# Small column tiles for the recurrence's levels in a two-layer hybrid encoder

## The chip, the cores and the metric

The kernel runs on one core of one Trainium2 chip. The metric is the device time of one execution in microseconds (us), as the median of a number of runs. The engines of the core are TensorE (matmul, in the profile as PE, its weight loads as PEld), VectorE (DVE), ScalarE (ACT), GpSimd (POOL) and SyncE (SP), which issues most transfers.

## The reference

The model has two layers over 512 tokens of width 1024, all in float32. Each layer mixes tokens in two groups of heads and then runs a gated convolutional feed-forward part:

```python
h = rms_norm(x, mix_norm_g[l])
proj = h @ w_in[l]                       # 1024 -> 4096
y_a = diff_attention(...)                # 4 heads, (softmax1 - lambda * softmax2) V
y_b = hgrn2_bidirectional(...)           # 4 heads, state 128 x 128, forward and backward
x = x + concat(y_a, y_b) @ w_out[l]
x = x + conv_glu_ffn(rms_norm(x, ffn_norm_g[l]), ...)   # 1024 -> 5632 -> 2816 -> 1024
```

The change is in the recurrence `y_b`. With forget gates f, keys k, values v and queries q per token it computes

```python
S_t = diag(f_t) S_{t-1} + k_t v_t^T ;  o_t = S_t^T q_t      # and the same backward, summed
```

Within a block of 128 tokens this is a matrix of scores A[s, t], in which key s and query t are multiplied with all forget gates that lie between them, and then A times v.

## The kernel before

**Columns.** A projection is cut into units: 128 output columns, a weight tile of 128 x 1024 in `raw`. ScalarE rounds it to `wH` (`high_now`, L893), POOL subtracts to get the rest `wL` (`split`, L491, in four pieces), and TensorE adds three products for each of the 8 slices (`triple`, L559 to L561): 24 matmuls of 128 x 512 a unit. `raw`, `wH` and `wL` have two buffers, so the split of unit s+1 is made while TensorE works on unit s, and unit s+1 can't start before it.

**Slots.** The mixing part of a layer is one hand-written list of 40 slots (L800). In each slot TensorE does, in this order: an item of the recurrence, the scores of an attention step, the first half of a unit's columns, then transposes of the attention weights W (`turn`, L717), the second half, a statistic (L609) and the attention's product with V (`values`, L726). Each other engine walks the same slots in an order of its own, and all wait on semaphores.

**The recurrence.** Heads go in pairs. A pair has 12 items, from slot 7 (pair 0) and slot 19 (pair 1). Item 0 computes the diagonal of A. Items 1 to 7 are levels: at level lv blocks of h = 2^(lv-1) tokens are joined in twos, and only the entries of A between two neighbouring blocks are new. For each level TensorE multiplies, for 2 heads and 4 blocks of 128 tokens, the keys `kx` (128 x 128, stationary) with the queries `QQ` (128 x 128, moving), which fills a bank of PSUM for each head (`item`, L612; L639 for the diagonal, L647 for h = 1, L650 for the other levels). Of the 128 x 128 results only the entries of a mask are kept.

Behind an item:
- POOL (`grow`, L505) waits for its last matmul (`lv_mm`), multiplies the totals (L518) and the keys KK (L524), and only then splits the next unit's weights (L491).
- ScalarE copies the grown keys to `kx` for the next level (L994).
- VectorE copies the masked entries to A (`masked`, L1394) and grows the queries QQ (L1415; at level 1 also the totals, L1424). In the same slot it takes a unit's result from PSUM (L1307), does the maximum of the scores (L1452), the weights W (`combine`, L1458 to L1463), squares (L1342) and rotary and norm work (L1319 to L1337).
- The next item waits for the queries (`hg_q`), the keys (`kx_ready`) and the masked copy (`a_msk`).

Items 8 to 11 turn the keys, carry the state from block to block and add all up (`to_keys`, `carry`, `gather`). The scores of the attention (`scores`, L708) are products of 64 rows: the two halves of the array hold the two softmaxes.

Of the kernel before, what the change touches and what calls it, by code (L numbers as in the profile page):

```python
# [11 lines left out]
ACT = mybir.ActivationFunctionType  # L12
AX = mybir.AxisListType

P = 128
D = 1024
S = 512
DEPTH = 2
HEADS = 4
# [2 lines left out]
EPS = 1e-6  # L22
KT = D // P
TT = S // P
FT = DFF // P


UNIT = KT * P
N_IN, N_OUT, N_UP, N_DOWN = 32, 8, 2 * FT, FT
U_OUT = N_IN  # L30
# [4 lines left out]

ROWS = FT - 4
U_TAIL = U_DOWN + ROWS
# [101 lines left out]
R_CONV = 26  # L139
NR = R_CONV + 8 * (FT + 2)  # L140

# [24 lines left out]
def build(nc, xT, wts, cst, msk, par, lbl, pos, outT):  # L166
# [15 lines left out]
    with ctx:  # L182
# [29 lines left out]
        KK = sb("KK", [P, 2, HEADS * S], F32, mix)  # L212
        A = sb("A", [P, 2, TT, P], F32, mix)
        KTOK = sb("KTOK", [P, 2, 2, TT - 1, P], F32, mix)
        ST = sb("ST", [P, 2, 2, TT - 1, P], F32, mix)
        QQ = sb("QQ", [P, 2, HEADS * S], F32, mix)
        T = sb("T", [P, 2, HEADS * S], F32, mix)
        HI = sb("HI", [P, TT, S], F32, mix)
        V = sb("V", [P, TT, S], F32, mix)
        QO = sb("QO", [P, HEADS, S], F32, mix)  # L220
        K2 = sb("K2", [P, 2, S], F32, mix)
        E = sb("E", [P, 2, S], F32, mix)
        wT = sb("wT", [P, 2, TT, P], F32, mix)
        kx = sb("kx", [P, 2, S], F32, mix)
# [6 lines left out]
        heads.close()  # L231
        gH = sb("gH", [P, FT * S], F32R, ffn)
        gL = sb("gL", [P, FT * S], F32R, ffn)
# [44 lines left out]
        kx_ready = signal("kx_ready", 14)  # L278
# [83 lines left out]

            return t[:, s, c * UNIT // 2:(c + 1) * UNIT // 2]

        def crossing(t, hd, i, h, left, n=1):


            side = HEADS * S * (1 if left == 0 else -1)
            return bass.AP(tensor=t[:].tensor, offset=left * HEADS * S + hd * S + i * P,
                           ap=[[2 * HEADS * S, P], [2 * h, n * P // (2 * h)], [side + h, 2], [1, h]])  # L370

        def neighbours(t, hd, i):


            return bass.AP(tensor=t[:].tensor, offset=hd * S + i * P,
                           ap=[[2 * HEADS * S, P], [HEADS * S + 1, 2], [2, P // 2]])

        def conv(p, c, n):

# [45 lines left out]
        with nc.Block() as block:  # L425
# [129 lines left out]
            def _(pe):  # L555
                for l in range(DEPTH):
# [55 lines left out]
                    def item(n):  # L612

                        pair, lv = divmod(n, PAIR_ITEMS)
                        if lv in (TURN_F, TURN_B):
                            to_keys(pair, lv - TURN_F)
                        if lv == CARRY:
                            carry(pair, 0)
                        if lv >= LEVELS:
                            return  # L620
                        pe.wait_ge(*hg_q.at(l, 9 * pair + lv + 1))
                        if lv:
                            pe.wait_ge(*kx_ready.at(l, 7 * pair + lv))
                        elif n == 0:
                            pe.wait_ge(*lam_exp.at(l, 1))
                        for r in range(2):
                            hd, b = 2 * pair + r, bank[2 + r]

                            if lv == 0:
                                if pair:  # L630
                                    pe.wait_ge(*oh_ready.at(l, r + 1))
                            elif lv == 1:
                                pe.wait_ge(*a_cp.at(l, 2 * pair + r + 1))
                            else:
                                pe.wait_ge(*a_msk.at(l, 14 * pair + 2 * (lv - 2) + r + 1))
                            for i in range(TT):
                                o = b[:, i * P:i * P + P]
                                if lv == 0:
                                    m = pe.matmul(o, kx[:, r, i * P:i * P + P], head(QQ, 1, hd, i, 1),  # L639
                                                  start=True, stop=True)  # L640
                                else:

                                    h = 2 ** (lv - 1)
                                    if h == 1:
                                        m = pe.matmul(o.rearrange("p (n two) -> p two n", two=2), kx[:, r, i * P:i * P + P],  # L647
                                                      neighbours(QQ, hd, i), start=True, stop=True)
                                        continue
                                    m = pe.matmul(o.rearrange("p (n two h) -> p n two h", two=2, h=h),  # L650
                                                  kx[:, r, i * P:i * P + P], crossing(QQ, hd, i, h, 0),
                                                  start=True, stop=True)
                            m.then_inc(lv_mm.sem, 1)

                    def to_keys(pair, d):
# [144 lines left out]
                    for s in range(SLOTS):  # L800
                        n = item_of(s)
# [60 lines left out]
                    for j in range(4):  # L862
                        pe.wait_ge(*w_split.at(l, U_TAIL + j + 1))
                        for c in range(2):
                            for k in range(4):
                                at = slice((ROWS + k) * S, (ROWS + k + 1) * S)
                                m = triple(bank[2 * j + c][:], j % 2, (2 * k + c) * P, gH[:, at], gL[:, at], False, k == 3)
# [3 lines left out]
            def _(act):  # L871
# [14 lines left out]
                for l in range(DEPTH):  # L886
# [83 lines left out]
                    def item(n):  # L970

                        pair, lv = divmod(n, PAIR_ITEMS)
                        if lv == 0:
                            for r in range(2):
                                act.wait_ge(*lv_mm.at(l, 16 * pair + r + 1))
                                if pair:
                                    act.wait_ge(*av_mm.at(l, r + 1))
                                act.activation(diag(r), bank[2 + r][:].rearrange("p (i t) -> p i t", i=TT), ACT.Copy)\
                                   .then_inc(a_cp.sem, 1)
                        if lv in (TURN_F, TURN_B):  # L980
                            d = lv - TURN_F
                            for r in range(2):
                                act.wait_ge(*kt_mm.at(l, 4 * pair + 2 * d + r + 1))
                                if pair:
                                    act.wait_ge(*kv_mm.at(l, 2 * d + r + 1))
                                act.activation(KTOK[:, r, d, :, :].rearrange("p n c -> p (n c)"), bank[2 + r][:, 0:3 * P], ACT.Copy)\
                                   .then_inc(kt_ready.sem, 1)
                        if lv <= 6:

                            act.wait_ge(*lv_mm.at(l, 16 * pair + 2 * lv + 2))  # L990
                            if lv:
                                act.wait_ge(*hg_k.at(l, 7 * pair + lv))
                            h = 2 ** lv
                            act.activation(kx[:].rearrange("p r t -> p (r t)").rearrange("p (n two h) -> p n two h", two=2, h=h),  # L994
                                           crossing(KK, 2 * pair, 0, h, 0, 2 * TT), ACT.Copy).then_inc(kx_ready.sem, 1)

                    def recurrent_out(pair):

# [647 lines left out]
```

## Time and profile before

| | us |
|---|---|
| median of 3 runs | 1389.43 (1387.84 to 1389.66) |
| the profiled execution | 1387.78 |
| its span | 1386.0 |
| TensorE busy in the span | 1369.8 |
| VectorE busy | 925.8 |
| POOL busy | 705.2 |
| ScalarE busy | 628.1 |

The profile is of one execution. Its span goes from the first to the last instruction; 1.78 us of the execution's time lie around it. Matmuls overlap each other, so the mean duration of one (390 ns for 512 columns of results) is longer than the step from one to the next. Busy shares are means over stages with different limits.

### The profile page before, as it was taken

The page shows a single profiled execution, that of the slowest core. Times are in us where ns is not written, and L with a number is a line of the kernel's source. Part 1 is how long each engine was busy: PE and PEld are TensorE (multiplying, and loading weights), DVE is VectorE, ACT ScalarE, POOL GpSimd, SP SyncE. Part 2 cuts the span into 40 slices and gives each one's busy share as a digit, 9 for nine tenths or more (in the row PEclk, how much of TensorE's full clock was granted, in tenths as well). Part 3 has the DMA queues.
Part 4 walks back from the last instruction along what each step waited for, and adds up shares of the span by engine and source line. Part 5 has one row for each costly group of instructions (what it writes and reads, how often), then busy time and mean ns, then how long its engine had stood idle before and what let it go on. Part 6 is the DMA issues. An engine that isn't in the chain of part 4 may idle for free.

```text
span 1386.0 us, 18086 instructions
## 1 busy us (share of the span) xinstructions
PE 1369.8 (99%) x6562; PEld 1119.9 (81%) x6562; DVE 925.8 (67%) x1078; ACT 628.1 (45%) x912; POOL 705.2 (51%) x539
## 2 busy tenths in 40 slices
PE   9999999999999999999999999999999999999999
PEld 6887787877888888888878877878778888888887
DVE  7687899555888888600356788985558888885001
ACT  6343666474544444312444426655745444443121
POOL 2785465337444444444567845552464444444443
PEclk9999999999999999999999999999999999999999
DMA  5223112122233233233332221221223333233233
GB/s 187 77 74 102 46 55 76 47 73 95 92 92 106 91 96 102 92 104 97 91 92 76 92 69 49 69 74 46 63 89 107 92 93 105 91 100 98 91 104 109
DMA packets 37130, 121.36 MB, mean 88 GB/s; under 512 B 4928, under 2 KB 5440, under 8 KB 37056
## 3 DMA queue, kind: packets, MB, share of 16 engines
q1 hardware_dynamic: 36768, 119.84, 27.9%
q8 instruction: 47, 0.77, 0.2%
q10 hardware_dynamic: 288, 0.52, 0.1%
q14 instruction: 27, 0.22, 0.1%
HBM read 114.05 MB, written 2.10 MB: 84 GB/s over the span
## 4 chain that ended last, share of the span: by engine, by line
PE 83%; DVE 6%; POOL 4%; ACT 4%; issue 3%; DMA 0%; ACTq 0%; POOLq 0%; DVEq 0%
PE bank L559 24%; PE bank L561 24%; PE bank L560 24%; PE bank L650 2%; PE bank L708 2%; PE bank L726 2%; POOL wL L497 1%; POOL KK L524 1%; PE bank L717 1%; DVE hL L399 1%; POOL rstd L411 1%; PE bank L681 1%; POOL wL L491 1%; ACT wH L893 1%; PE bank L647 1%
## 5 line engine op out<-in xcount | busy, mean ns | idle before, releaser
L497 POOL TENSOR_TENSOR wL<-raw,wH 128x1024 fp32r<-128x1024 f32 x142 | 343.1, 2416 | 404.4 <-ACT wH L893 294.2
L559 PE MATMUL bank<-hH,wH 128*128 128x512 f32 x1216 | 483.1, 397 | 2.6 <-POOL wL L491 1.3
L561 PE MATMUL bank<-hL,wH 128*128 128x512 f32 x1216 | 474.4, 390 | 0.0
L560 PE MATMUL bank<-hH,wL 128*128 128x512 f32 x1216 | 473.7, 390 | 0.0
L491 POOL TENSOR_TENSOR wL<-raw,wH 128x256 fp32r<-128x256 f32 x268 | 240.1, 927 | 186.7 <-ACT wH L893 186.6
L559 PEld LDWEIGHTS bank<-hH,wH 128*128 128x128 f32 x1216 | 228.3, 188 | 66.4 <-issue 16.3
L561 PEld LDWEIGHTS bank<-hL,wH 128*128 128x128 f32 x1216 | 228.2, 188 | 48.7
L560 PEld LDWEIGHTS bank<-hH,wL 128*128 128x128 f32 x1216 | 228.6, 188 | 45.4 <-issue 0.5
L893 ACT ACTIVATE wH<-raw 128x1024 fp32r<-128x1024 f32 x173 | 182.6, 1055 | 154.4 <-PE bank L561 154.1
L1567 DVE TENSOR_TENSOR x<-x,bank 128x512 f32<-128x512 f32 x16 | 10.9, 683 | 200.7 <-PE bank L561 200.7
L559 PE MATMUL bank<-gH,wH 128*128 (+1 forms) x352 | 137.2, 390 | 0.0
L561 PE MATMUL bank<-gL,wH 128*128 (+1 forms) x352 | 136.9, 389 | 0.0
L560 PE MATMUL bank<-gH,wL 128*128 (+1 forms) x352 | 136.9, 389 | 0.0
L1554 DVE TENSOR_TENSOR gL<-gt,gH 128x512 fp32r<-128x512 f32 x44 | 99.6, 2264 | 30.8 <-ACT gH L1146 30.8
L1541 DVE SCALAR_TENSOR_TENSOR ua<-uu,R,ua 128x511 f32<-128x511 f32 x44 | 111.4, 2531 | 1.5
L901 ACT ACTIVATE wH<-raw 128x1024 fp32r<-128x1024 f32 x36 | 38.1, 1059 | 146.4 <-PE bank L561 146.4
L1135 ACT ACTIVATE ua<-uu,R 128x512 f32<-128x512 f32 x44 | 35.9, 816 | 126.8 <-DVE uu L1532 126.8
L1532 DVE TENSOR_TENSOR uu<-bank,rms 128x512 f32<-128x512 f32 x88 | 59.9, 684 | 44.9 <-PE bank L561 26.9
L524 POOL TENSOR_TENSOR KK<-KK,T 128x512 f32<-128x512 f32 x56 | 74.5, 1352 | 25.2 <-PE bank L647 25.2
L559 PEld LDWEIGHTS bank<-gH,wH 128*128 128x128 f32 x352 | 66.1, 188 | 14.5 <-issue 0.7
L561 PEld LDWEIGHTS bank<-gL,wH 128*128 128x128 f32 x352 | 66.1, 188 | 13.7
L560 PEld LDWEIGHTS bank<-gH,wL 128*128 128x128 f32 x352 | 66.1, 188 | 13.6
(173 smaller groups left out, 1801.2 us busy)
## 6 DMA issues: line engine op xcount, KB each, us to landing
raw<-wts SPq DMA_DIRECT2D x210, 512.0 KB, 3.5
x<-xT SPq DMA_DIRECT2D x8, 256.0 KB, 5.2
swp<-K SPq DMA_DIRECT2D x32, 64.0 KB, 2.0
swp<-QO SPq DMA_DIRECT2D x32, 64.0 KB, 2.2
outT<-x SPq DMA_DIRECT2D x8, 256.0 KB, 2.0
raw<-wts ACTq DMA_DIRECT2D x2, 256.0 KB, 4.4
raw<-wts SPq DMA_DIRECT2D x2, 256.0 KB, 5.4
W<-pos SPq DMA_DIRECT2D x1, 256.0 KB, 5.8
```

Source lines behind the costliest of these rows:

```text
L491: m = pool.tensor_tensor(wL[:, s, at], raw[:, s, at], wH[:, s, at].bitcast(F32), ALU.subtract)
L497: pool.tensor_tensor(wL[:, s, :], raw[:, s, :], wH[:, s, :].bitcast(F32), ALU.subtract)\
L524: last = pool.tensor_tensor(v, v, w.to_broadcast([P, n, h]), ALU.mult)
L559: pe.matmul(out, wH[:, s, a:a + P], rhs_h, start=first, stop=False)
L560: pe.matmul(out, wL[:, s, a:a + P], rhs_h, start=False, stop=False)
L561: return pe.matmul(out, wH[:, s, a:a + P], rhs_l, start=False, stop=last)
L893: act.activation(wH[:, u % 2, :], raw[:, u % 2, :], ACT.Copy).then_inc(w_high.sem, 1)
L901: act.activation(wH[:, s, :], raw[:, s, :], ACT.Copy).then_inc(w_high.sem, 1)
L1135: act.activation(dst[:, q, :], uu[:, q, c, :], ACT.Identity, bias=conv(p, c, 3), scale=conv(p, c, 1))\
L1532: dve.tensor_tensor(uu[:, p % 2, c, :], bank[(2 * p + c) % 4][:], rms[:], ALU.mult).then_inc(up_ev.sem, 1)
L1541: dve.scalar_tensor_tensor(dst[:, q, 0:S - 1], uu[:, q, c, 1:S], conv(p, c, 2), dst[:, q, 0:S - 1], ALU.mult, ALU.add).then_inc(conv_done. ...
L1554: dve.tensor_tensor(gL[:, at], gt[:, p % 2, :], gH[:, at].bitcast(F32), ALU.subtract)\
```

## The change

For levels 1 to 7 each product of a 128 x 128 block is replaced by products of smaller blocks on the diagonal. Where the joined blocks (2h tokens) fit into 32 tokens, so for levels 1 to 5 (h = 1 to 16), there are four, each with 32 keys as stationary columns and 32 queries as moving columns; their results lie at PSUM partitions 0, 32, 64 and 96, so at four column quarters of the array. For level 6 (h = 32) there are two of 64 by 64, and for level 7 (h = 64) two of 64 by 64 off the diagonal: the keys of one half with the queries of the other. All contract over the 128 rows as before. The diagonal (item 0), the semaphores and the other engines' instructions stay; ScalarE's copy to `kx` calls the same helper with other arguments and does the same.

```diff
+SUB, QUARTER = P // 2, P // 4
...
-        def crossing(t, hd, i, h, left, n=1):
+        def crossing(t, hd, i, h, left, g=None):
             side = HEADS * S * (1 if left == 0 else -1)
-            return bass.AP(tensor=t[:].tensor, offset=left * HEADS * S + hd * S + i * P,
-                           ap=[[2 * HEADS * S, P], [2 * h, n * P // (2 * h)], [side + h, 2], [1, h]])
+            at, n = g or (0, 2 * S)
+            return bass.AP(tensor=t[:].tensor, offset=left * HEADS * S + hd * S + i * P + at,
+                           ap=[[2 * HEADS * S, P], [2 * h, n // (2 * h)], [side + h, 2], [1, h]])
-        def neighbours(t, hd, i):
-            return bass.AP(tensor=t[:].tensor, offset=hd * S + i * P,
-                           ap=[[2 * HEADS * S, P], [HEADS * S + 1, 2], [2, P // 2]])
+        def neighbours(t, hd, i, g):
+            return bass.AP(tensor=t[:].tensor, offset=hd * S + i * P + g * QUARTER,
+                           ap=[[2 * HEADS * S, P], [HEADS * S + 1, 2], [2, QUARTER // 2]])
+        def across(t, hd, i, g):
+            at = hd * S + i * P + g * SUB
+            return t[:, g, at:at + SUB]
...
-                                else:
-                                    h = 2 ** (lv - 1)
-                                    if h == 1:
-                                        m = pe.matmul(o.rearrange("p (n two) -> p two n", two=2), kx[:, r, i * P:i * P + P],
-                                                      neighbours(QQ, hd, i), start=True, stop=True)
-                                        continue
-                                    m = pe.matmul(o.rearrange("p (n two h) -> p n two h", two=2, h=h),
-                                                  kx[:, r, i * P:i * P + P], crossing(QQ, hd, i, h, 0),
-                                                  start=True, stop=True)
+                                    continue
+                                h = 2 ** (lv - 1)
+                                sub = QUARTER if 2 * h <= QUARTER else SUB
+                                for g in range(P // sub):
+                                    s, at = kx[:, r, i * P + g * sub:i * P + (g + 1) * sub], slice(g * sub, (g + 1) * sub)
+                                    if h == SUB:
+                                        m = pe.matmul(o[at, (1 - g) * SUB:(2 - g) * SUB], s, across(QQ, hd, i, 1 - g),
+                                                      start=True, stop=True)
+                                    elif h == 1:
+                                        m = pe.matmul(o[at, at].rearrange("p (n two) -> p two n", two=2), s,
+                                                      neighbours(QQ, hd, i, g), start=True, stop=True)
+                                    else:
+                                        m = pe.matmul(o[at, at].rearrange("p (n two h) -> p n two h", two=2, h=h), s,
+                                                      crossing(QQ, hd, i, h, 0, (g * sub, sub)), start=True, stop=True)
                             m.then_inc(lv_mm.sem, 1)
...
-                                           crossing(KK, 2 * pair, 0, h, 0, 2 * TT), ACT.Copy).then_inc(kx_ready.sem, 1)
+                                           crossing(KK, 2 * pair, 0, h, 0), ACT.Copy).then_inc(kx_ready.sem, 1)
```

## Rows read from the trace of the kernel before

**Rows 1.** The page: TensorE's busy time, share, instructions; the chain by engine.

```profile
PE 1369.8 (99%) x6562; PEld 1119.9 (81%) x6562; DVE 925.8 (67%) x1078; ACT 628.1 (45%) x912; POOL 705.2 (51%) x539
...
PE 83%; DVE 6%; POOL 4%; ACT 4%; issue 3%; DMA 0%; ACTq 0%; POOLq 0%; DVEq 0%
```

**Rows 2.** One line's instructions: durations in ns, minimum, median, maximum.

```profile
L650 PE MATMUL bank<-QQ,kx x384: 270/275/348, 61.5 to 910.3; 128*128 128x128 f32 x192
```

**Rows 3.** TensorE's timeline, level 5 of pair 0: start us, duration us.

```profile
85.32 0.39 PE L561 MATMUL bank<-hL,wH 128*128 128x512 f32 x1
85.55 1.95 PE L650 MATMUL bank<-QQ,kx 128*128 128x128 f32 x16
...
87.57 0.40 PE L560 MATMUL bank<-hH,wL 128*128 128x512 f32 x1
```

**Rows 4.** Timeline at an L708; counts in 0.04 us (TensorE, loads).

```profile
146.43 0.28 PE L639 MATMUL bank<-QQ,kx 128*128 128x128 f32 x1
146.64 0.70 PE L708 MATMUL bank<-K,QO 64*128 64x512 f32 x2
...
148.04 0.40 PE L560 MATMUL bank<-hH,wL 128*128 128x512 f32 x1
...
146.63:146.66 0.03, 0.02 (x2) 0.02 (x2) 1.00 0.47 137
...
147.16:147.20 0.04, 0.04 (x4) 0.00 (x0) 1.00 0.86 205
```

**Rows 5.** Timeline at L573, and its durations in ns.

```profile
22.71 1.02 PE L568 MATMUL bank<-rstd,C 128*128 128x512 f32 x2
23.57 0.28 PE L573 MATMUL bank<-lamc,C 128*128 128x2 f32 x2
...
L573 PE MATMUL bank<-lamc,C x4: 167/209/251, 23.6 to 710.8; 128*128 128x2 f32 x4
```

**Rows 6.** L650's weight loads; TensorE's first stand for the split.

```profile
L650 PEld LDWEIGHTS bank<-QQ,kx x384: 186/192/192, 61.3 to 910.2; 128*128 128x128 f32 x192
...
63.98 0.47 PE L559 MATMUL bank<-hH,wH 128*128 128x512 f32 x1 [0.39 <-POOL wL L491]
```

**Rows 7.** POOL's timeline, pair 0; its waits to 102: us, times, longest.

```profile
56.26 3.45 POOL L524 TENSOR_TENSOR KK<-KK,T 128x512 f32<-128x512 f32 x2 [3.13 <-PE bank L647]
59.67 4.16 POOL L491 TENSOR_TENSOR wL<-raw,wH 128x256 fp32r<-128x256 f32 x4
63.78 1.67 POOL L518 TENSOR_TENSOR T<-T 128x256 f32<-128x256 f32 x2
...
68.41 2.81 POOL L491 TENSOR_TENSOR wL<-raw,wH 128x256 fp32r<-128x256 f32 x4
...
POOL T L518 <- PE bank L650: 2.8, 3, 1.5
```

**Rows 8.** The same waits in layer 1, from 743 to 783.

```profile
POOL T L518 <- PE bank L650: 4.1, 4, 1.5
```

**Rows 9.** A slot of pair 1: length, busy PE, PEld, DVE, ACT, POOL; clock.

```profile
165.90:177.20 11.30, 10.70 (x60) 8.22 (x60) 11.09 (x17) 6.18 (x11) 7.14 (x8) 1.00 0.27 80
```

**Rows 10.** Waits: VectorE from 156.3 to 223.5, TensorE from 158.3 to 221.3.

```profile
DVE sm L1452 <- PE bank L708: 0.7, 2, 0.3
...
DVE A L1394 <- PE bank L650: 0.2, 1, 0.2
...
PE bank L717 <- DVE W L1463: 0.3, 1, 0.3
```

**Rows 11.** W made ready on VectorE and turned on TensorE, pair 1's level 5.

```profile
203.32 1.11 DVE L1463 SCALAR_TENSOR_TENSOR W<-E,sm 128x512 f32<-128x512 f32 x1
...
204.66 0.60 PE L717 MATMUL bank<-C,W 128*128 128x128 f32 x4
```

**Rows 12.** The weights' transfers: count, KB each, us to landing.

```profile
raw<-wts SPq DMA_DIRECT2D x210, 512.0 KB, 3.5
```

**Rows 13.** TensorE's longest waits in layer 1, columns as in rows 9.

```profile
815.00:823.00 8.00, 5.38 (x27) 3.50 (x26) 7.61 (x21) 3.43 (x7) 1.24 (x2) 1.00 0.26 87
```

## The prediction, made before the changed kernel was run

> **What bounds the kernel now.** I read the shares and the chain of waits first, then TensorE's groups by form, its order of time around single items, and then POOL and VectorE in the stretches in which the recurrence runs. TensorE is busy for 99% of the span and has 83% of the chain [rows 1]: time taken from it shortens the kernel, unless another engine is late there. The changed products are 384 of the 6562 TensorE records under L650, 192 products in two records each [rows 2]: 2 layers, 2 pairs of heads, levels 2 to 7, 8 products. Level 1 adds 64 under L647. So an item (one level of one pair) is 8 products in 16 records. Its price is read from the steady matmuls about it, not from the duration of 275 ns, since matmuls overlap: the last column matmul before it starts at 85.32, the second after it at 87.57; with 0.23 for each column matmul the item takes 87.57 - 0.23 - 85.55 = 1.79 us [rows 3]. That is 0.11 a record. The 28 items of levels 1 to 7 are 50 us, 3.6% of the span of 1386.0; 20 of them become quarters, 8 halves.
>
> **What replaces an item.** A quarter item issues four products of 128 rows, 32 columns and 32 tokens for each old one: 64 weight loads and 64 matmuls. A half item issues 32 and 32. Nothing before shows a column tile, so I bound it.
> - Below: the four quarters run side by side and each takes a matmul in 28 ns. That is the start-to-start of L573's two matmuls of 2 columns: the pair covers 0.28 us and the second alone 0.251 [rows 5]. 16 in each quarter are 0.45 us.
> - Middle: the quarters take turns, 64 x 0.028 = 1.79 us: what it was.
> - Above: each small pair costs what a whole one does, 64 x 0.11 = 7.0 us.
>
> The nearest row for the choice is L708, the two half-height products of the scores (64 rows each): two matmuls of 0.69 us each start together and are both over in 0.70, and both second passes start in the same 0.04 us [rows 4]. Tiles of the array do run side by side for float32, and two loads and two matmuls go out within 0.03 us, so issue is no bound of 28 ns either. I take the lower bound plus a third for 128 instructions: 0.6 us. Halves: 16 in each half at half of 0.11, 0.9 us.
>
> **Switches of tiling.** They are in the trace, at L708. In: L639's last matmul starts at 146.43 and would leave the array after 0.11; L708 starts at 146.64, 0.10 later than that [rows 4]; and a first weight load then lies bare, 0.1 for 128 columns, 0.02 for 32. Out: the second pass starts at 147.18, is worth 0.43 (two take 23.57 - 22.71 [rows 5]), and L560 starts at 148.04 where 147.18 + 0.43 + 0.23 = 147.84 was due: 0.20. So a quarter item pays 0.12 in and 0.20 out. In pair 1 the scores follow at once and L708 pays its switch today already, so only 0.12 is new.
>
> The Trainium skill says the same of the switch ("TensorEngine Tiling (Array Packing)", Key Properties: a change of tiling mode drains TensorE), and its section Instruction Overhead warns against taking the tiling factor from a dimension that is small already, since a matmul with few columns lasts as long as one with 60. Here the moving size falls from 128 to 32, so that rule speaks against this change: its figure of 60 cycles gives an estimate of 0.025 us for each of 64, 1.6 us in turn. By it the item gains nothing; side by side the same floor gives 0.4.
>
> **Sum on TensorE alone.** Pair 0: quarter item 0.12 + 0.6 + 0.20 = 0.92, saves 0.87, five times; half item 0.12 + 0.9 + 0.20 = 1.22, saves 0.57, twice: 5.5 us a layer. Pair 1: 0.72 and 1.02, saves 1.07 and 0.77: 6.9 a layer. Both layers: 24.8 us. I don't expect it, because two other engines are just behind.
>
> **Pair 0: POOL.** In each slot POOL waits for the item's last matmul, grows the keys, then splits the next unit's weights, for which TensorE waits. In layer 0 POOL runs without a gap from 56.26 (released by L647) to 71.2, and TensorE stands for the split at 63.98 and once more, at 79.52 [rows 6, 7]: grow and split take 63.78 - 56.26 = 7.5 us there, a slot's 24 column matmuls 24 x 0.227 = 5.45. With items of 0.9 TensorE's slot is 6.4 and POOL sets the pace. What POOL gives back: the start after item 1 (about 1.0 earlier) and its three gaps, 2.8 us with 1.53 the longest [rows 7]: 3.8 us at most. Stepping both engines through levels 1 to 7 with POOL's durations kept, TensorE reaches the columns after level 7 3.6 us early. In layer 1 there are four gaps, 4.1 us [rows 8], and the same stepping gives 3.6. POOL's splits take 2.8 us alone and up to 4.2 beside VectorE [rows 7, 8]; filled gaps mean more overlap, so I take 3.4 a layer, 6.8. ScalarE's copies to kx come ready before the columns end, at level 3 up to 0.3 after; that is in the stepping.
>
> **Pair 1: VectorE.** Of five slots of 10.3 to 11.3 us VectorE is busy in each for all but 0.1 to 0.6 (11.09 of 11.30 in the fullest, records overlapping a little [rows 9]). From 156.3 to 223.5 it waits 1.1 us in all, at the two ends, and TensorE waits for its W once [rows 10]. An item shorter by 1.07 makes TensorE's slot 9.3 to 9.7, less than VectorE's work. What can move: VectorE's two waits at the head, 0.17 before L1394 and 0.33 before L1452, so some 0.5; then the products are turned (L717) as soon as W is ready, and for the turn at 204.66 W was done at 204.43, a slack of 0.2 [rows 11]. There TensorE can be 0.7 early. The two half items behind add 0.77 each while VectorE gets back 0.16 + 0.34, the like two waits behind level 7 [rows 10]; the turn at 235.00 has its W at 233.97, 1.0 before. So min(0.7 + 1.5, 1.05 + 1.0) = 2.0 us a layer, 4.0 in all; the other 9.8 become waits before L717 and the items. Behind that VectorE has gaps of several us and TensorE is the bound again, so what is gained by then stays.
>
> In layer 1 VectorE is also full between pair 0's last level and the first scores, and TensorE stands still there for 2.6 of 8 us [rows 13]; that work starts from level 7's item and moves with it, so I subtract nothing. PSUM's other columns hold old sums, which the masks leave out; VectorE, POOL and ScalarE have the same instructions. Weight transfers land after 3.5 us [rows 12] and are asked for a slot of about 7 us ahead; they stay hidden. The granted clock is 1.00 (2.4 GHz) even in those 8 us [rows 13], and the new waits are shorter.
>
> **Sum.** 6.8 + 4.0 = 10.8 us. The profiled execution took 1387.78, span 1386.0 and 1.78 about it; it becomes 1377.0. The median of the runs, 1389.43, lies 1.65 above it: predicted 1378.6. The result's own range: with items of 0.8 and POOL not slowed, 13.5 less (1376); with items of 1.2 and each bound tighter by a third, 7 less (1382.5).
>
> **Rivals.**
> - Quarters take turns. A quarter item is 1.79 + 0.12 + 0.20 = 2.11, a half item (32 x 0.056) + 0.32 the same: 0.32 more than before in pair 0, 0.12 in pair 1. Pair 0: seven items 2.2, of which 0.2 falls into TensorE's waits for the split; pair 1: 0.8. A layer 2.9, in all 5.8: 1395.2, slower. It decides from 23 ns for a small pair counted over all quarters: (1.79 - 0.32) / 64. For it: the quarters read the same 128 rows, L708's halves different ones. Against: the overlap at L708. 15%.
> - A small pair costs what a whole one does or nearly: items of 3.5 to 7.2. All 28 at 1.7 more are 48 us: 1437; at 5.3 more, over 1500. For it: 0.11 is the step of every run of pairs in the rows. Against: L573's 28 ns. 5%, 2 of them for this: where a load can't lie beside a matmul of the same rows, a pair is 0.11 / 4 + 0.028 and an item 3.5. The Trainium skill has that as a rule ("TensorE: Matmul & The Clock Gate", The mechanism: loads overlap matmuls only in another row group). The trace speaks against it: L650's loads last 0.19 each at a step of 0.11 beside matmuls of the same rows [rows 2, 6].
> - Overlap of two instead of four (both bounds met half way): quarter item 0.12 + 1.0 + 0.20, saves 0.47 in pair 0 and 0.67 in pair 1. POOL and VectorE then bind less: 1.7 and 1.2 a layer, in all 5.8: 1383.6. 9%.
> - It does run side by side, but the other engines give back nearly nothing (POOL slowed by what the gaps gave): within 3 us, 1387. 5%.
>
> **How the numbers follow.** Forecast 66%, the rivals 15, 5, 9 and 5. 0.2% is 2.8 us, about what can be told from no change. Faster: 66 + 8 of the third, 1 of the fourth, less 3 for what I overlooked, 72%. Same: 10%. Slower: 13 of the first, 5 of the second: 18%. The likeliest's own range is 1376 to 1382.5; the range of all reaches over the third, fourth and first: 1374.5 to 1396.
>
> **What would show it.** Starts of small matmuls under the new lines 7 to 10 ns apart across quarters, an item of 0.7 to 0.9 us from last column matmul to next; POOL without gaps from level 1 to 6 of pair 0, and TensorE waiting for wL (L491) in five or six slots a layer instead of one or two; in pair 1 new waits of TensorE for VectorE (W, QQ, A). The prediction is wrong if items are over 1.5 us, if a clock under 1.00 shows there, or if VectorE's work turns out to shrink.

## The result, and the profile after

| | before | changed |
|---|---|---|
| median of the runs, us | 1388.64 (4 runs, 1387.84 to 1389.66) | 1376.32 (4 runs, 1375.31 to 1377.66) |
| ratio, 95% interval | | 0.9911 (0.9894 to 0.9929) |
| profiled execution, us | 1387.78 | 1376.25 |
| its span, us | 1386.0 | 1374.5 |
| mean granted clock | 1.000 | 0.998 |

The kernel became 12.3 us faster by the medians and 11.5 by the spans of the profiles; 10.8 was forecast, and 1378.6 as the time. Lines of the changed kernel stand 7 to 9 further down than in the kernel before: the column matmuls at L566 to L568 (L559 to L561), `to_tokens` at L601 (L594), the scores at L717 (L708), the turn of W at L726 (L717). Some experiments shift them once more. First the page of the changed kernel, the lines that answer to [rows 1]:

```profile
PE 1346.1 (98%) x7650; PEld 1091.3 (79%) x7650; DVE 918.4 (67%) x1078; ACT 628.6 (46%) x912; POOL 709.3 (52%) x539
...
PE 72%; DVE 13%; POOL 5%; issue 5%; ACT 4%; DMA 0%; DVEq 0%; ACTq 0%; POOLq 0%
```

TensorE has 1088 instructions more and 23.7 us of busy time less; half of that is in the span. The rest has become waits: 13% of the chain lies on VectorE instead of 6%. POOL and VectorE have as many instructions as before, but VectorE's take 7.4 us less in all.

**The item.** TensorE's timeline at a quarter item (level 5 of pair 0, to be held against [rows 3]) and at a half item (level 7 of pair 0). Columns: start us, duration us.

```profile
83.87 0.39 PE L568 MATMUL bank<-hL,wH 128*128 128x512 f32 x1
84.19 0.76 PE L660 MATMUL bank<-QQ,kx 128*32 128x32 f32 x64
84.88 0.51 PE L566 MATMUL bank<-hH,wH 128*128 128x512 f32 x1
85.22 0.39 PE L567 MATMUL bank<-hH,wL 128*128 128x512 f32 x1
...
97.99 0.40 PE L617 MATMUL bank<-sqR,meanR 128*128 128x512 f32 x1
98.31 1.15 PE L654 MATMUL bank<-QQ,kx 128*64 128x64 f32 x32
99.40 0.50 PE L566 MATMUL bank<-hH,wH 128*128 128x512 f32 x1
99.73 0.39 PE L567 MATMUL bank<-hH,wL 128*128 128x512 f32 x1
```

By the prediction's own way of reading, the quarter item takes 85.22 - 0.23 - (83.87 + 0.23) = 0.89 us (1.79 before, 0.92 forecast) and the half item 99.73 - 0.23 - (97.99 + 0.23) = 1.28 (1.22 forecast). The switch in is 84.19 - 84.10 = 0.09; the first small matmul starts there, and the 64 starts cover 0.567 us, which is 9.0 ns from one to the next and 36 in each quarter, on the mean. In the first half of the item the trace has them in rounds: four starts 6 to 7 ns apart, one for each quarter, and the next four 32 ns after them (53 ns at the very first round); in the second half the order is less regular, about 34 ns for four. The 32 starts of a half item cover 0.93 us, 30 ns each.

**Pair 0.** POOL's waits, in layer 0 from 54.4 to 99 and in layer 1 from 735 to 780, to be held against [rows 7, 8] (us in total, times, longest):

```profile
POOL KK L531 <- PE bank L657: 2.0, 1, 2.0
POOL T L525 <- PE bank L660: 0.6, 2, 0.5
...
POOL T L525 <- PE bank L660: 1.7, 2, 1.0
```

The gaps of 2.8 and 4.1 us between POOL's levels have shrunk to 0.6 and 1.7. In exchange TensorE waits, in the whole span:

```profile
PE bank L566 <- POOL wL L498: 6.1, 6, 1.4
PE bank L601 <- DVE ev L1316: 3.7, 7, 1.2
PE bank L717 <- DVE QO L1334: 3.7, 2, 1.8
PE bank L726 <- DVE W L1472: 2.4, 2, 1.2
```

The first of them (1.3 us before) is the split of pair 0. The second, but for 0.3 us that was there before, and the third are VectorE in pair 1; before the change TensorE waited 0.3 us a layer there for QO and never for `ev`. L601 is `to_tokens`, for which VectorE takes the projection from PSUM to `ev` (L1316); QO is the rotated query of the attention's scores. The wait for W, which the prediction named, has gone down from 3.1 to 2.4 us, and in pair 1 from 0.3 us a layer to nothing.

**Pair 1.** VectorE has one wait of 0.2 us in the 81.4 us from 150.6 to 232 (busy 80.02). TensorE's timeline at the longest of its waits there, and two stretches in the columns of [rows 9] (length, busy PE, PEld, DVE, ACT, POOL, granted clock), one in each layer:

```profile
164.13 1.39 PE L717 MATMUL bank<-K,QO 64*128 64x512 f32 x4 [1.83 <-DVE QO L1334]
165.45 0.80 PE L566 MATMUL bank<-hH,wH 128*128 128x512 f32 x1
166.04 0.63 PE L567 MATMUL bank<-hH,wL 128*128 128x512 f32 x1
166.47 0.63 PE L568 MATMUL bank<-hL,wH 128*128 128x512 f32 x1
...
168.47 0.39 PE L567 MATMUL bank<-hH,wL 128*128 128x512 f32 x1
...
164.90:168.30 3.40, 3.40 (x9) 2.27 (x8) 3.33 (x3) 2.08 (x3) 3.40 (x4) 0.50 0.31 77
847.50:850.90 3.40, 3.40 (x8) 1.61 (x9) 3.29 (x5) 1.41 (x3) 3.40 (x4) 0.51 0.23 58
```

TensorE stands for 1.83 us, and behind that the granted clock is half (1.2 GHz instead of 2.4) for 3.41 us: column matmuls start 0.43 apart instead of 0.23. The same is found in layer 1.

**Stage by stage.** The start of TensorE's first matmul of a stage in the trace after, less that before:

| stage | shift at its start | at its end | the stage | forecast |
|---|---|---|---|---|
| pair 0, layer 0 | +0.21 | -3.36 | -3.57 | -3.4 |
| pair 1, layer 0 | -3.36 | -5.69 | -2.33 | -2.0 |
| pair 0, layer 1 | -5.77 | -9.16 | -3.39 | -3.4 |
| pair 1, layer 1 | -9.16 | -11.50 | -2.34 | -2.0 |

Between and behind these stages nothing moves by more than 0.1 us. The 0.2 us ahead of the first belong to the program's start, where TensorE's first waits differ.

**How the runs scatter.** Some executions of the kernel before take 1389.3 to 1389.7 us (mean clock 0.999), the others 1387.4 to 1388.2 (1.000). No trace of the first kind is kept of this very kernel; in before_mask1's, which took 1389.20, the clock falls once, in the middle of layer 1, behind a stand (the last section shows it). So its median moves by up to 1.5 us with the mixture. Medians below are set against 1387.95 (19 runs, for the first four experiments), 1387.93 (15, the next four), 1389.32 (7, the next three) and 1388.14 (3, the last). Where it matters I compare two traces instead, by how far the starts of TensorE's matmuls shift over a stage.

### The profile page after: what moved, and what is told of

The parts are those of the page before. It is cut to its first block, busy times and chain, and to the rows that moved or that the text cites. A ratio compares the mean times of both kernels' runs of the same rounds, so it can differ in the third digit from the quotient of the medians.

```text
span 1374.5 us, 20262 instructions
## 1 busy us (share of the span) xinstructions
PE 1346.1 (98%) x7650; PEld 1091.3 (79%) x7650; DVE 918.4 (67%) x1078; ACT 628.6 (46%) x912; POOL 709.3 (52%) x539
## 4 chain that ended last, share of the span: by engine, by line
PE 72%; DVE 13%; POOL 5%; issue 5%; ACT 4%; DMA 0%; DVEq 0%; ACTq 0%; POOLq 0%
PE bank L566 22%; PE bank L568 22%; PE bank L567 22%; DVE QQ L1424 2%; POOL KK L531 2%; POOL wL L504 1%; DVE A L1403 1%; DVE sm L1461 1%; POOL wL L498 1%; DVE E L1469 1%; PE bank L717 1%; DVE sqR L1351 1%; DVE hL L406 1%; DVE tmp L1328 1%; DVE swp L1330 1%
## 5 line engine op out<-in xcount | busy, mean ns | idle before, releaser
L566 PE MATMUL bank<-hH,wH 128*128 128x512 f32 x1216 | 484.3, 398 | 8.7 <-POOL wL L498 6.1
L568 PE MATMUL bank<-hL,wH 128*128 128x512 f32 x1216 | 475.0, 391 | 0.0
L566 PEld LDWEIGHTS bank<-hH,wH 128*128 128x128 f32 x1216 | 228.9, 188 | 73.0 <-issue 16.0
L568 PEld LDWEIGHTS bank<-hL,wH 128*128 128x128 f32 x1216 | 228.7, 188 | 49.3
L566 PE MATMUL bank<-gH,wH 128*128 (+1 forms) x352 | 137.2, 390 | 0.0
L568 PE MATMUL bank<-gL,wH 128*128 (+1 forms) x352 | 136.9, 389 | 0.0
L566 PEld LDWEIGHTS bank<-gH,wH 128*128 128x128 f32 x352 | 66.1, 188 | 14.3 <-issue 0.6
L568 PEld LDWEIGHTS bank<-gL,wH 128*128 128x128 f32 x352 | 66.1, 188 | 13.9
```

What stands on the lines that cost most here:

```text
L566: pe.matmul(out, wH[:, s, a:a + P], rhs_h, start=first, stop=False)
L568: return pe.matmul(out, wH[:, s, a:a + P], rhs_l, start=False, stop=last)
```

## The experiments

**Do the quarters run side by side?** same_quarter gives all four products of a block the same column quarter, and keeps their number and size (the sums of the levels are not the reference's); the half items stay as they are:

```diff
-    m = pe.matmul(o[at, at].rearrange(...), s, crossing(QQ, hd, i, h, 0, (g * sub, sub)), ...)
+    m = pe.matmul(o[0:sub, at].rearrange(...), s, crossing(QQ, hd, i, h, 0, (g * sub, sub)), ...)   # levels 1 to 5
```

> Built on the changed kernel. All four small products of a block at levels 1 to 5 write to PSUM partitions 0 to 31, so all use one column quarter of the array; count, sizes and order of the instructions stay. Their results overwrite what the masks would keep, so the levels' sums are left out. Theory (the quarters run side by side, 36 ns a pair in each, 64 x 9 ns in all): in one quarter 64 pairs follow each other at about 36 ns (28 at the least), an item's starts cover 1.8 to 2.3 us instead of 0.57, items grow by 1.2 to 1.7 us, and the kernel is no faster than the one before: 1388 to 1396. Rival (the price of a small pair is one of issue, 9 ns wherever it goes): items stay at 0.57 and the time at 1376.

quarter_by_quarter keeps the quarters, but issues the four blocks of one quarter behind each other, so that 8 records of a quarter follow each other. The same loop puts the records of the half items in rows of 8 of one half:

```diff
-    for i in range(TT):
-        for g in range(P // sub):
+    for g in range(P // sub):
+        for i in range(TT):
```

> Built on the changed kernel. Same products, another order: for each head first the four blocks of quarter 0, then those of quarter 1, and so on, so that 8 pairs (16 instructions) of one quarter stand in a row. Theory A (TensorE looks far enough ahead to feed four quarters from such a row): items 0.6 to 0.8 us of starts, time 1376 to 1378. Theory B (matmuls start in the order of the program, so a quarter's row must end before the next begins): starts 64 x 28 to 36 ns, 1.8 to 2.3 us, time 1388 or more. In the changed kernel two pairs of a quarter stand in a row already and cost nothing.

Measured: 1390.0 us (ratio 1.0011, 1.0000 to 1.0022) and 1382.75 (0.9957, 0.9941 to 0.9972). TensorE's timeline at level 5 of pair 0, first same_quarter, then quarter_by_quarter:

```profile
86.62 2.21 PE L660 MATMUL bank<-QQ,kx 128*32 128x32 f32 x64
88.76 0.50 PE L566 MATMUL bank<-hH,wH 128*128 128x512 f32 x1
```

```profile
84.87 1.51 PE L661 MATMUL bank<-QQ,kx 128*32 128x32 f32 x64
86.31 0.50 PE L566 MATMUL bank<-hH,wH 128*128 128x512 f32 x1
```

Same work, three prices: the 64 starts cover 2.02 us in one quarter (32 ns each), 1.32 in four with eight of one quarter in a row (21 ns), and 0.567 in turn (9.0 ns). The gain of the quarter items is overlap between quarters and nothing else: without it the kernel is no faster than before. In a row of one quarter the starts are 32 ns apart (the first two 53), and from round to round in the changed kernel they are 32 to 34: three neighbours hardly slow a quarter down.

The second run lies between the two theories. If records of different quarters overlapped freely wherever they stand in the program, it would be as fast as the change. Its starts show how far the overlap reaches: a row of 8 begins 0.153 us behind the one before it, 6 ns after the fifth record of that row, when three are still to start. So here quarters overlapped over the last three records of a row, and no further. Part of this run's loss is that of the half items: in rows of one half their starts cover 1.32 us instead of 0.93.

**What each part brings.** pair0_only leaves pair 1 the whole products, halves_only leaves them to levels 1 to 5 of both pairs:

```diff
     sub = QUARTER if 2 * h <= QUARTER else SUB
+    if pair == 1:        # pair0_only
+    if lv <= 5:          # halves_only
+        sub = P
```

> Built on the changed kernel. Pair 1's levels are whole products as before, pair 0's are small. Theory (pair 0 gives 3.57 and 3.39 us in the two layers up to POOL's pace, pair 1's part is its own): 7.0 us less than the kernel before, 1381.7, and the granted clock stays at 1.00 in pair 1's level 2, since TensorE's item is long enough that it doesn't stand before the scores. Rival (an earlier pair 0 moves VectorE's and POOL's work so that pair 1 gives or takes too): 5 or less, or 9 or more.

> Built on the changed kernel. Levels 1 to 5 are whole products as before, levels 6 and 7 are halves. Theory: a half item takes 1.1 us instead of 1.79 (0.7 less in pair 0, where both switches of tiling are new, 0.8 less in pair 1). In pair 0 POOL has 1.5 us to give behind level 5, so both items count: 1.4; in pair 1 VectorE is late by 0.5 at the most behind level 5, both count: 1.6. 3.0 a layer, 5 to 6 in all: 1383. Rival (behind level 5 the split's or VectorE's lateness takes one of the two): 3 in all, 1386.

Measured: 1382.13 us (0.9953, 0.9931 to 0.9976) and 1384.13 (0.9970, 0.9959 to 0.9981). With pair 0 alone the two stages bring 3.56 and 3.34 us, as in the change (3.57 and 3.39), pair 1 has its old waits of 0.3 us, and its clock stays at 1.00. So the two pairs add up: the trace is 6.9 us shorter than that of the kernel before, where 7.0 were expected. The medians say 5.8; two of this kernel's three runs have a mean clock of 0.999. The half items alone bring 2.0 us a layer, 0.8 in pair 0 and 1.2 in pair 1, where TensorE alone would give 1.0 and 1.6: less than the 3.0 of my theory and more than the rival's 1.5. Part of them is taken by the same two engines (POOL in pair 0, VectorE in pair 1: a wait of 0.2 before L601 is new).

**Is POOL the bound in pair 0?** after_split3 and before_split3 leave the last quarter of the split out for seven units of each layer, in pair 0's slots, in the changed kernel and in the one before (two of the 24 products of each of these units take an old wL there):

```diff
-    for q in range(4):
+    for q in range(3 if 9 <= u <= 15 else 4):
```

> Built on the changed kernel. POOL leaves out one of four pieces of the split for units 9 to 15, the ones split in pair 0's slots (a quarter of those units' low weights is stale). POOL is 0.9 to 1.0 us shorter in each of these slots. Theory (POOL sets the pace in pair 0: TensorE's seven items save 5.9 us a layer there and it keeps 3.4 to 3.6): most of the other 2.4 a layer comes back, 3.5 to 5 us less than the changed kernel: 1372. Rival (something else, the keys' copy on ScalarE or VectorE's queries, is late as well): under 1.5 us less.

> The same piece left out in the kernel before. There TensorE stands for the split three times, 0.39, 0.54 and 0.39 us. Theory: 1 to 1.5 us less than the kernel before, 1387.4. Rival (any POOL work taken off the stretch helps alike, also in the changed kernel): 4 us less here too.

Measured: 1372.91 us (0.9888, 0.9860 to 0.9917; two runs, the profiled one with a fall of the clock more than the change's) and 1385.75 (0.9983, 0.9972 to 0.9995). Against its own base the changed kernel gains 2.08 and 1.82 us in pair 0 of the two layers; the kernel before gains 0.8 and 0.2 there, and 1.2 more in layer 1, where TensorE's wait of 0.8 us before the carry goes. So the same relief of POOL is worth about 3.9 us in pair 0 after the change and 1.0 before: POOL, a near bound before, is the bound now. Both theories were a little off: 3.4 us by the medians of the changed kernel for the 3.5 to 5 expected, 2.2 in the kernel before for 1 to 1.5, still about half of the rival's 4.

**Is VectorE the bound in pair 1?** after_mask1 and before_mask1 copy only one block of four from PSUM to A in pair 1 (three quarters of the levels' entries of A are missing there), so that the two copies of 0.69 us in each slot take 0.25 each:

```diff
-    dve.copy_predicated(diag(r), m, bank[2 + r][:].rearrange("p (i t) -> p i t", i=TT))
+    dve.copy_predicated(diag(r)[:, 0:nb, :], m, ...[:, 0:nb, :])      # nb = 1 if pair else TT
```

> Built on the changed kernel. VectorE's masked copies of pair 1 take one block of 128 tokens instead of four (three quarters of the scores of pair 1 stay those of the diagonal). VectorE is about 1.0 us shorter in each of seven slots. Theory (VectorE is without a gap from level 1 of pair 1 on and TensorE loses 4.9 us a layer to it, 1.1 of them through the clock that falls while it stands): 7 to 9 us less than the changed kernel, 1368; clock 1.00 throughout. Rival (the loss is one of contention or of the switches of tiling): under 2 us less.

> The same copies shortened in the kernel before, where TensorE waited for VectorE in pair 1 for 0.35 and 0.25 us a layer. Theory: 1 to 1.5 us less than the kernel before, 1387.3. Rival: as much as in the changed kernel.

Measured: 1374.75 us (0.9901, 0.9873 to 0.9930; two runs) and 1388.64 (0.9999, 0.9988 to 1.0011; one of its eight runs took 4894.24, for which there is no trace, and the median of the other seven is 1388.10). The kernel before doesn't move, as expected: there VectorE has slack. The changed one gains 1.1 us in pair 1 of layer 0 and 1.8 in layer 1, where a fall of the clock is missing; the fall in layer 0 stayed, at 165.6 us. 7 to 9 were expected, so the number is the rival's, under 2 us by the medians. My reckoning by busy time was wrong. VectorE's timeline at level 1 of pair 1, after_mask1 and then the changed kernel:

```profile
152.91 0.50 DVE L1404 COPY_PREDICATED A<-M,bank 128x128 f32<-128x128 uint8 x2
153.85 1.29 DVE L1462 TENSOR_REDUCE sm<-bank 128x1 f32<-128x512 f32 x2 [0.44 <-PE bank L717]
155.06 1.34 DVE L1351 TENSOR_TENSOR sqR<-sq,sqR 128x512 fp32r<-128x512 f32 x1
```

```profile
152.80 1.37 DVE L1403 COPY_PREDICATED A<-M,bank 128x512 f32<-128x512 uint8 x2
154.06 1.27 DVE L1461 TENSOR_REDUCE sm<-bank 128x1 f32<-128x512 f32 x2
155.25 1.04 DVE L1351 TENSOR_TENSOR sqR<-sq,sqR 128x512 fp32r<-128x512 f32 x1
```

The copies lose 0.87 us, but behind them VectorE waits 0.44 for the scores of this slot, and its next instruction is 0.30 longer. What is left at L1351's end is 0.0. The wait for QO is 1.83 us as before. What is shortened ahead of the scores' maximum is not on the path; that runs from the scores to the maximum, squares, queries, totals, rotary work and so to the next scores. VectorE is full, and yet only the work behind one point in each slot counts. The rival's cause, contention, has a part too: seven times 0.87 us is 6.1, but the busy time of the same VectorE instructions falls by only 4.5 us a layer.

**Work on that path, and its neighbour.** totals_pool moves the totals of level 1 of pair 1 from VectorE to POOL, behind its split; the result stays the same. They take 2.25 us on VectorE, just ahead of the rotary work. totals_both in addition moves the totals of level 2 of pair 0 the other way, from POOL to VectorE:

```diff
+    def pair_totals(pair):                      # POOL, called for pair 1 (item 1)
+        pool.wait_ge(*hg_q.at(l, 9 * pair + 3))
+        ...
+            nxt = pool.tensor_tensor(totals(pair, 2)[:, d, :], w[:, :, 0], w[:, :, 1], ALU.mult)
+        nxt.then_inc(tot_ready.sem, 1)
-    if lv == 1:                                 # VectorE
+    if lv == 1 and not pair:
```

> Built on the changed kernel, whole computation. The totals of level 1 of pair 1 (two products of 128 x 512, 2.25 us on VectorE) are made on POOL, behind its split, where it stands 2.06 us for TensorE's next item. What shortening the masked copies showed: work of VectorE ahead of the maximum of the scores gives little (its time went to a wait of 0.44 for the scores and to slower instructions beside POOL); these totals lie behind it, on the way to the rotated queries for which TensorE stands 1.83 us before the next scores. Theory (that way sets the time of the slot, and the fall of the clock follows from the stand): the 1.83 goes, the clock stays at 1.00 in level 2, and the later waits for ev (0.33 and 1.22) shrink: 2 to 3 us a layer, 1371 (1370 to 1373). Rival (POOL's longer work, 3 us or more in a gap of 2, makes the keys or the split late, or slows VectorE by as much): 0 to 1.5 us, 1375 or more.

> The same, and in pair 0 the totals of level 2 (1.67 us on POOL) are made on VectorE, which is busy for 4.6 of 8.2 us in that slot. Theory (POOL sets pair 0's pace): 1 to 1.5 us a layer less than with the totals of pair 1 alone, 1368.5. Rival (VectorE's own items behind, the next queries or the totals for level 3, become late): no more than 1 us in all, 1370 to 1371.

Measured: 1374.53 us (0.9898, 0.9882 to 0.9915) and 1373.89 (0.9892, 0.9875 to 0.9908). The first gains 0.95 us a layer in pair 1, not 2 to 3: the rival's range, though its time lies a little under the rival's 1375. VectorE's timeline ahead of the scores' QO, in totals_pool (with POOL's row for the same time behind it) and in the changed kernel:

```profile
158.25 1.22 DVE L1339 SCALAR_TENSOR_TENSOR tmp<-QO,R,cosT 128x512 f32<-128x512 f32 x1
159.51 1.11 DVE L1341 SCALAR_TENSOR_TENSOR swp<-swp,R,sinT 128x512 f32<-128x512 f32 x1
160.65 1.41 DVE L1343 TENSOR_TENSOR QO<-tmp,swp 128x512 f32<-128x512 f32 x1
162.10 1.41 DVE L1345 TENSOR_TENSOR QO<-QO,rstd 128x512 f32<-128x512 f32 x1
...
160.03 2.93 POOL L540 TENSOR_TENSOR T<-T 128x512 f32<-128x512 f32 x2
```

```profile
158.63 2.25 DVE L1433 TENSOR_TENSOR T<-T 128x512 f32<-128x512 f32 x2
160.81 0.74 DVE L1328 SCALAR_TENSOR_TENSOR tmp<-QO,R,cosT 128x512 f32<-128x512 f32 x1
161.58 0.75 DVE L1330 SCALAR_TENSOR_TENSOR swp<-swp,R,sinT 128x512 f32<-128x512 f32 x1
162.37 0.69 DVE L1332 TENSOR_TENSOR QO<-tmp,swp 128x512 f32<-128x512 f32 x1
163.09 0.99 DVE L1334 TENSOR_TENSOR QO<-QO,rstd 128x512 f32<-128x512 f32 x1
```

The four instructions take 5.15 us here and 3.17 in the changed kernel: 1.98 of the 2.25 us come back. They now start 2.6 us earlier, so that the first two run nearly all beside POOL's split (until 160.06) and the last two beside the totals; in the changed kernel POOL stands from 160.34 to 162.40. The second move adds 0.6 us a layer in pair 0, at the bound that after_split3 showed: about half of the theory's 1 to 1.5, and its 1368.5 was far off. It is the fastest version here with the whole computation, 2.4 us under the change by the medians.

**The stand at level 2 of pair 1.** level2_whole gives that one item of each layer the whole products back. after_split3_pair1 shortens the split for pair 1's units instead, made beside VectorE's work (two products of each of these units take an old wL again):

```diff
+    if pair == 1 and lv == 2:                   # level2_whole
+        sub = P
-    for q in range(4):                          # after_split3_pair1
+    for q in range(3 if 20 <= u <= 27 else 4):
```

> Built on the changed kernel, whole computation. Only level 2 of pair 1 is whole products again, so TensorE works 1.1 us longer there and stands 0.7 instead of 1.8 us before the scores. Theory (the fall of the clock to half in that slot, 3.4 us, follows from TensorE's stand and costs 1.1 us a layer, since the columns behind it run at half speed): the fall goes in both layers, 2 us less than the changed kernel, 1374.3. Rival (the fall comes for another reason, the small tiles' low activity over the whole stretch, or costs nothing since VectorE is late anyway): 1376 as it was.

> Built on the changed kernel. POOL leaves out one of four pieces of the split for units 20 to 27, the ones split beside pair 1's levels (a quarter of those units' low weights is stale). TensorE never waits for POOL there, and POOL stands for 1.4 to 4.8 us in each slot. Theory (VectorE sets the pace of pair 1 and is slowed by POOL's work beside it, about 0.4 us for each us: with the totals moved to POOL the four rotary instructions took 5.15 us instead of 3.17, which gave back what the move saved): with 1.0 to 1.2 us less of POOL in each of eight slots VectorE gains some 0.4 a slot, and 1 to 2 us a layer come off, 1373 (1371.5 to 1374.5). Rival (POOL isn't late there, so its work costs nothing): within 0.7 us of the changed kernel, or no more than the fall of the clock in level 2 explains (1.1 a layer).

Measured: 1376.1 us (0.9907, 0.9891 to 0.9924) and 1372.86 (0.9887, 0.9858 to 0.9916; two runs). TensorE's timeline at the same scores, first level2_whole, then after_split3_pair1:

```profile
163.78 1.13 PE L719 MATMUL bank<-K,QO 64*128 64x512 f32 x4 [0.33 <-DVE QO L1336]
164.83 0.50 PE L566 MATMUL bank<-hH,wH 128*128 128x512 f32 x1
```

```profile
163.64 1.13 PE L717 MATMUL bank<-K,QO 64*128 64x512 f32 x4 [1.32 <-DVE QO L1334]
...
166.43 0.39 PE L567 MATMUL bank<-hH,wL 128*128 128x512 f32 x1
```

The slower item costs nothing: the scores start 0.35 us earlier than in the change (0.1 of it comes from before the stage), since QO was what they waited for, and the clock stays up behind a stand of 0.33. The next item starts 1.3 us earlier. Of that 1.0 is given back at the next wait for `ev` (level 4) and 0.6 won again at the two waits behind it; 0.9 us a layer stay, no more. This trace has a fall elsewhere, at 812.3 us (1.5 us), so its time hardly differs from the change's; its one run at clock 1.000 took 1374.52, the change's 1375.31. The theory's mechanism held, a short stand and no fall behind it, but its 2 us didn't come: 0.2 us by the medians, 0.8 at equal clock.

In after_split3_pair1 the stand is 1.32 us and the clock stays up too. It gains 1.83 and 1.74 us a layer. From L717 to the eighth column matmul behind it the changed kernel loses 1.55 us by the clock (168.47 - 164.13 = 4.34 against 166.43 - 163.64 = 2.79), of which TensorE would otherwise wait 0.4 for W. So at that place the fall costs about 1.1. At the end of the layer it is worth less, since VectorE takes part of it back: the changed kernel's own run at clock 1.000 took 1375.31, its two at 0.998, the clock of the profile with its two falls, 1376.25 and 1376.38, which is 1.0 us for two falls (one run against two; the fourth, at 0.997, took 1377.66). Both runs here are at clock 1.000 and 2.4 us under that 1375.31. So about 1.2 of the 1.8 us a layer is not the clock but VectorE being faster beside a shorter split: the totals of level 1, 2.25 us long in the change, take 1.71, and the same instructions of pair 1 take 2.4 and 2.1 us less in the two layers. The rival, that only the clock would change, is 1.2 us a layer short.

## Why the prediction was right

- **Quarters side by side (forecast 66%).** Item 0.89 us for 0.92, half item 1.28 for 1.22. The sum is nearer than its parts: a quarter's step is 32 ns and not L573's 28, the first is 53, and on the mean it is 36. That the third added for safety makes 37 is luck. The switches, 0.12 in and 0.20 out from [rows 4], measure 0.09 in and, with the last record's own time, 0.89 - 0.09 - 0.57 = 0.23 out.
- **The rivals on the price.** Turns were priced at 1.79 us of starts. same_quarter built just that, 2.02, and the kernel was only 2.1 us slower than the one before, not 5.8, since its half items stayed cheap and part of the rest fell into waits. Whole prices (7 us an item) and an overlap of two (1.0) are out. So is the rule cited from the Trainium skill, that weights load beside matmuls of another row group only ("TensorE: Matmul & The Clock Gate", The mechanism): with it an item was 3.5 us, and here all quarters read the same rows. Its floor for a matmul with few columns ("TensorEngine Tiling (Array Packing)", Instruction Overhead), from which I estimated 1.6 us in turn and 0.4 side by side, is the nearer one: 2.02 in one quarter, 0.57 over four. A floor of this kind shows within a quarter (32 ns, for the 25 of the estimate), not over the four together (9.0 ns).
- **Pair 0, POOL: 3.4 a layer forecast, 3.57 and 3.39 measured.** The stepping held. Its picture of where TensorE would wait was too even: three waits of up to 1.4 us a layer, not five or six. POOL's own durations didn't grow as its gaps filled.
- **Pair 1, VectorE: 2.0 a layer forecast, 2.33 and 2.34 measured.** The engine was right and the place wrong. I took the turn of W as the point that binds, from a slack of 0.2 us [rows 11]. TensorE stood for QO at level 2 and for `ev` at `to_tokens` (L601). A wait for QO was in the trace before, once a layer in pair 1, and I stepped past it:

```profile
PE bank L708 <- DVE QO L1325: 0.3, 1, 0.3
```

  With 6.95 us a layer saved in the items, 4.6 are lost: 1.5 at QO, 1.0 by the clock, 2.1 at three waits for `ev`. That the sum came out near 2.0 is partly luck. The cap of 2.05 was too tight: level2_whole gains 3.2 us a layer over the kernel before in this stage and after_mask1 4.2 in the layer without a fall, though there VectorE also has less to do. The falls, which I had put at nothing, took part of what went over the cap.
- **The clock.** "The granted clock is 1.00 ... and the new waits are shorter" is the step that failed, and a clock under 1.00 was one of my own signs that the prediction is wrong. In the stretch of [rows 13] the clock was 1.00 although TensorE stands there for 1.7 us at once, and eight other traces show a fall behind that very stand, before_mask1's among them, whose TensorE has the same work. One execution at 1.00 was no evidence that there is none. A new stand of 1.83 us was followed by half clock for 3.41 us in both layers: 1.0 to 1.1 us at the place, about 0.5 a layer in the kernel's time. Another of my signs showed as well: VectorE's busy time fell, from 925.8 to 918.4 us with the same 1078 instructions.
- **The missing 1.5 us.** 10.8 forecast, 11.5 in the spans: +0.2 in pair 0, +0.7 in pair 1. The medians differ by 0.8 more, as the kernel before has a fall in two of its four runs. The time itself, 1376.32 for 1378.6, is off by 0.8 more again, because the median before is now 1388.64 and was 1389.43; it lies at the lower end of the likeliest range.

What stays open: why the clock falls behind a stand in one place and not in another. Stands of 1.3 to 1.5 us at level 2 of pair 1 (totals_pool, totals_both, after_split3_pair1) had no fall in six cases. Stands of 1.83 (the change, after_split3, after_mask1) had one in five of six: in layer 1 of after_mask1 the same stand passed at full clock. And the stand of 1.7 us in the middle of layer 1 is followed by a fall in 8 of the 14 traces.

## What to carry to other kernels

Small products on a block diagonal pay on TensorE when their results go to different column quarters and the program takes the quarters in turn: read the price from the starts, and lay out the loop so that neighbours differ in quarter. A saving on the busiest engine is worth what the next one leaves of it: step both engines through the stage, with the gaps of the second as the cap, and look for the point in each slot behind which its work counts. A new stand on TensorE can cost more than itself, by the clock behind it: here 1.83 us did, in most cases.

## What the runs showed of the hardware

**Order within the array.** 64 loads and 64 matmuls of 128 rows, 32 columns and 32 tokens in float32 cost 0.57, 1.32 or 2.02 us by the order and place of their quarters alone. Within a quarter the step is 32 ns with the other three idle, 32 to 34 with all four busy.

**VectorE beside POOL.** The same rotary instructions take 0.74, 0.75, 0.69 and 0.99 us with POOL idle for half of the time and 1.22, 1.11, 1.41 and 1.41 beside its split and its totals. Moving 2.25 us of work from one to the other brought 0.27 on the spot.

**The clock behind a stand.** The kernel of before_mask1, whose TensorE has the work of the kernel before, in the middle of layer 1: its timeline, and a stretch in the columns of [rows 9]:

```profile
817.06 1.90 PE L681 MATMUL bank<-HI,KTOK 128*128 128x128 f32 x12 [0.86 <-DVE ST L1444]
820.71 1.13 PE L708 MATMUL bank<-K,QO 64*128 64x512 f32 x4 [1.75 <-ACT E L1016]
...
822.30:825.70 3.40, 3.40 (x9) 2.63 (x8) 3.33 (x6) 0.34 (x1) 2.81 (x4) 0.50 0.14 34
```

After stands of 0.86 and 1.75 us the clock is at half for 3.41 us and the kernel ends 1.5 us later than where the same stands pass without it. All falls in the middle of these traces last 3.41 us.
